# Second mixer's output: the last chunk of the first four weight tiles gets a place of its own

## The chip, the cores and the metric

One core of one Trainium2 chip. The metric is the time of one execution in device microseconds. The profile gives the span of one execution, with the activity of TensorE (PE; PEld is its weight load), VectorE (DVE), ScalarE (ACT), GpSimd (POOL), and of SyncE (SP), which only issues transfers here.

## What is computed

The reference is a network of two transformer blocks in float32 over 512 tokens of width 1024 (`D_MODEL = 1024`, `SEQ = 512`). The first block has two layers, the second one. The place of the change is the first block's second layer, whose mixer joins a multi-scale pooling with a stick-breaking attention of four heads and multiplies the result by one square matrix:

```python
def cd_mixer(h, w_in, pool_w, pool_scale, q_norm, k_norm, w_out):
    B, S, _ = h.shape
    u, sq, sk, sv = split_cols(h @ w_in, CD_SPLITS)
    o_pool = multiscale_pool(u, pool_w, pool_scale)
    q = rms_norm(sq.reshape(B, S, SB_HEADS, SB_HEAD_DIM), q_norm)
    k = rms_norm(sk.reshape(B, S, SB_HEADS, SB_HEAD_DIM), k_norm)
    v = sv.reshape(B, S, SB_HEADS, SB_HEAD_DIM)
    o_sb = stick_breaking_attention(q, k, v)
    mix = jnp.concatenate([o_pool, o_sb.reshape(B, S, -1)], axis=-1)
    return mix @ w_out
```

Then `x = x + g1 * y`, a normalisation that depends on the condition vector, and the SwiGLU feed-forward, whose first matrix is w1.

## The kernel before

**Layout.** Everything is feature-major: a chunk is 128 features (partitions) by 512 tokens, and a tensor of width 1024 is eight chunks. Products are float32 accurate by splitting each operand in an upper and a lower half and making three matmuls of each product (`products`, L391 to L393): upper weights by `hi`, upper weights by `lo`, lower weights by `hi`.

**The weight stream.** Weights come as a stream of units of 128 x 1024 floats (512 KB), in the order of use. A unit of the mixer's output matrix holds the eight 128 x 128 blocks of one output tile. SP's queue fills a ring of four places, `ring`, in order: for each unit it waits until TensorE has let go the unit four before it (`emptied`), then issues the transfer (L1273). GpSimd (`split_unit`) waits for the transfer, writes `uppers` (L1857), waits for that, and writes `lowers` over the ring's own place (L1860). TensorE waits for `lower_made`. So a ring place cannot be refilled before the last matmul that reads its lower half.

**The second mixer's output** (`second_mix_out`). Eight output tiles in two passes of four. Tile q of a pass adds up in PSUM bank q. The first pass is woven into the rest of the attention: the attention's work is cut in parts 0 to 31, which all engines go through in the same order (`sb_part(h)` on TensorE, a loop over `h` on ScalarE and VectorE). Parts 24 to 27 are each followed by chunks 0 to 3 of a tile (in the order 1, 2, 0, 3); part 28 by chunks 4 and 5 of tiles 0 and 1; part 29 by those of tiles 2 and 3; part 30 (`sb_outputs` of head 3, L518) by chunk 6 of all four, and then chunk 7 of all four, behind which each unit is let go. The second pass takes four new units, eight chunks each. Chunk 4 + n is head n's output: PSUM to SBUF on ScalarE (`cd_mixed`), then VectorE's split, `cd_split`: a cast (L2452) and a subtraction (L2453), both inside SBUF, tied to each other by a semaphore (`link`).

**VectorE's order at the end.** For head 3: the subtraction of L2473, the four products of `sb_weights` (L2480, two operands in SBUF, 128 x 128), for which TensorE's part 30 waits (`sb_w`); the split of head 3's chunk; `make_coef` (L1923, L1928, L1929: three operations on 8 columns, inside SBUF); then `residual`, over chunks k of 0 to 7: `xres` from the finished tile (L1975, one operand in PSUM); ScalarE's square and scaled copy; `raw_split` (L1936, L1937, which read PSUM); `sum_square` (L1946 or L1949).

**Behind it.** The feed-forward's first tile (`raw_tile`) starts with 16 small matmuls (L436), before which TensorE waits until seven squares are summed (`x_summed`), and then goes through the chunks as `x_raw` comes.

Of the kernel before, what the change touches and what calls it, by code (L numbers as in the profile page):

```python
# [31 lines left out]
F32 = mybir.dt.float32  # L32
F32R = mybir.dt.float32r
I32 = mybir.dt.int32
ALU = mybir.AluOpType
ACT = mybir.ActivationFunctionType
AX = mybir.AxisListType.X

P = 128
D = 1024  # L40
KC = D // P
# [5 lines left out]
RING = 4  # L47
# [91 lines left out]
def build(nc, A, plan):  # L139

    ctx = ExitStack()
    with ctx:
# [5 lines left out]
        def sem(name):  # L148
            if name not in sems:
                sems[name] = ctx.enter_context(nc.semaphore(name))  # L150
            return sems[name]
# [37 lines left out]
        def f32r(name, at, *dims):  # L189

            return nc.alloc_sbuf_tensor_at(name, [P, *dims], F32R, offset=at).ap()
# [94 lines left out]
                     ("lb", 4, S), ("w", 4, S), ("gap3", 2, S), ("u", 4, SM))  # L286
        poolw = L1["poolw"]
        B1 = L1
        cd_half = f32r("cd_half", big_at + 4 * AFTER_UPPERS, 30, S)

        def cd_mixed(k):
# [3 lines left out]
        def cd_halves(k):  # L295
            return (cd_half[:, 26 + k, :], cd_half[:, 22 + k, :]) if k < 4 else (cd_half[:, k, :], cd_half[:, k - 4, :])
# [34 lines left out]
        shift_uses = {"f0": 1, "n1": 2, "f1": 3}  # L331
        full_count = {}
        by_unit = {}

        def ready(eng, name, i=None):

            b, k = uses[name]
            if name in by_unit:
                read, n, step = by_unit[name]
                eng.wait_ge(read, n if i is None else i * step + n)  # L340
            else:
                eng.wait_ge(full[b], full_count[name])
            return b
# [19 lines left out]
        def _(pe):  # L363
# [24 lines left out]
            def products(out, s, k, hi, lo, start, stop):  # L388

                upper, lower = uppers[:, s, k * P:(k + 1) * P], lowers[:, s, k * P:(k + 1) * P]  # L390
                pe.matmul(out, upper, hi, start=start, stop=False)  # L391
                pe.matmul(out, upper, lo, start=False, stop=False)  # L392
                return pe.matmul(out, lower, hi, start=False, stop=stop)  # L393
# [145 lines left out]
            def second_mix_out():  # L539

                stream("cd_out", 0, KC)
                slot = ring_loop(2, 4)
                take = bank_loop(2, range(4), [("m1", "y", q) for q in range(4)])

                def chunks(i, q, order):
                    for k in order:
                        if i == 0:
                            pe.wait_ge(sem("m1_split"), k + 1)
                        mm = products(ps[:, q, :], (loop["base"] + q) % RING, k, *cd_halves(k), k == 0, k == KC - 1)
                    return mm  # L550
                for n, q in enumerate((1, 2, 0, 3)):
                    sb_part(24 + n)
                    take(0, q)
                    slot(0, q)
                    chunks(0, q, range(4))
                for n in range(2):
                    sb_part(28 + n)
                    for q in (2 * n, 2 * n + 1):
                        chunks(0, q, range(4, 6))
                sb_part(30)  # L560
                for q in range(4):
                    chunks(0, q, range(6, 7))
                for q in range(4):
                    chunks(0, q, range(7, 8)).then_inc(emptied[(loop["base"] + q) % RING], 1)
                for q in range(4):
                    take(1, q)
                    s = slot(1, q)
                    chunks(1, q, range(KC)).then_inc(emptied[s], 1)

            def tm_group(name, off, meta=None, first=4, between=None):  # L570

# [44 lines left out]
            def bank_loop(n_iter, banks, names, per_result=1):  # L616


                base = {}
                for n, (b, name) in enumerate(zip(banks, names)):  # L620
                    uses[name] = (b, nuse[b])
                    u = loop["base"] + (n + 1) * per_result - 1
                    by_unit[name] = (emptied[u % RING], u // RING + 1, loop["step"])
                    base[b] = nuse[b]
                    nuse[b] += n_iter

                def take(i, b):
                    pe.wait_ge(drained[b], i + base[b])
                return take
# [631 lines left out]
        @block.sync  # L1261
        def _(sp):
            for n in range(n_first):
                by = "rows" if n % ADA_FIRST >= 2 else "sums"
                sp.dma_start(first_w[n], stream_dram[n, :, :]).then_inc(sem(f"first_{by}_filled{n // ADA_FIRST}"), 16)
            sp.dma_start(small_unit, stream_dram[n_first, :, :]).then_inc(sem("small_unit_loaded"), 16)
            for s in range(RING):
                sp.dma_start(ring[:, s, :], stream_dram[n_first + 1 + s, :, :]).then_inc(filled[s], 16)
            sp.dma_start(consts[:, 0:FREQS_AT], A["consts"][:, 0:FREQS_AT]).then_inc(sem("consts_loaded"), 16)
            with sp.Fori(1, n_ring // RING) as i:  # L1270
                for s in range(RING):
                    sp.wait_ge(emptied[s], i)
                    sp.dma_start(ring[:, s, :], stream_dram[i * RING + (n_first + 1 + s), :, :]).then_inc(filled[s], 16)  # L1273
            for s in range(n_ring % RING):
                sp.wait_ge(emptied[s], n_ring // RING)
                sp.dma_start(ring[:, s, :], stream_dram[n_units - n_ring % RING + s, :, :]).then_inc(filled[s], 16)
            for k in range(KC):
                sp.wait_ge(sem("x_out"), k + 1)
                sp.dma_start(A["out"][:, k, :], hbuf[:, k, 0:S]).then_inc(sem("stored"), 16)
            sp.wait_ge(sem("stored"), 16 * KC)  # L1280

        @block.scalar
        def _(act):
# [356 lines left out]
            def sb_exps(hd, tiles, name):  # L1640

                was_drained(act, ("aft", hd, name))
                for j in tiles:
# [2 lines left out]
                        ready(act, ("so", hd - 1))  # L1646
                    f(L1["w"][:, j, 0:w], L1["lb"][:, j, 0:w], ACT.Exp).then_inc(sem("sb_e"), 1)
            for h in range(SB_ENDS):
                if h - 3 in POOL_AT:
                    g = POOL_AT.index(h - 3)  # L1650
                    b = ready(act, ("py", g))
                    drain(f(cd_mixed(g), ps[:, b, :], ACT.Copy, scale=V("pool_scale", g)), b)
                if h % 2 == 0 and h // 2 - 1 in SQK_SLOTS:
                    sqk_square(SQK_SLOTS.index(h // 2 - 1))
                if h == 12:
                    for i in range(NT):
                        b = ready(act, ("sv", i))
                        drain(f(L1["sv"][:, i, :], ps[:, b, :], ACT.Copy), b)
                if h - 2 in SB_AT:
                    hd = SB_AT.index(h - 2)  # L1660
                    sb_exps(hd, (3, 2), (3, 2))
                    sb_exps(hd, (1,), (1,))
                if h - 3 in SB_AT:
                    sb_exps(SB_AT.index(h - 3), (0,), (0,))
                if h in SB_AT:
                    sb_log(SB_AT.index(h))
                if h in SB_OUT_AT:
                    hd = SB_OUT_AT.index(h)
                    b = ready(act, ("so", hd))
                    drain(f(cd_mixed(4 + hd), ps[:, b, :], ACT.Copy), b)  # L1670
                if h % 2 and (h - 3) // 2 in SQK_SLOTS:
                    sqk_rstd(SQK_SLOTS.index((h - 3) // 2))
# [206 lines left out]
        def _(dve):  # L1879
# [597 lines left out]
            def sb_weights(hd, tiles):  # L2477
                for j in tiles:
                    dve.wait_ge(sem("sb_e"), NT * hd + NT - j)
                    tt(L1["w"][:, j, 0:P], L1["w"][:, j, 0:P], C("strict"), ALU.mult).then_inc(sem("sb_w"), 1)  # L2480
            for h in range(SB_ENDS):
                if h - 2 in SB_AT:
                    hd = SB_AT.index(h - 2)
                    sb_subtract(hd, (3, 2))
                    sb_subtract(hd, (1,))
                if h - 3 in SB_AT:
                    hd = SB_AT.index(h - 3)
                    sb_subtract(hd, (0,))
                    sb_weights(hd, (3, 2, 1, 0))
                if h - 1 in SB_AT:  # L2490
                    sb_parts(SB_AT.index(h - 1))
                if h in POOL_AT:
                    pool_window(POOL_AT.index(h))
                if h - 4 in POOL_AT:
                    g = POOL_AT.index(h - 4)
                    was_drained(dve, ("py", g))
                    cd_split(g)
                if h - 1 in SB_OUT_AT:
                    hd = SB_OUT_AT.index(h - 1)
                    was_drained(dve, ("so", hd))  # L2500
                    cd_split(4 + hd)
                if h % 2 and (h - 3) // 2 in SQK_SLOTS:
                    sqk_scale(SQK_SLOTS.index((h - 3) // 2))
# [324 lines left out]
```

## Time and profile before

| | us |
|---|---|
| median of 3 runs | 2572.9 |
| lowest, highest | 2569.6, 2574.5 |
| the profiled execution | 2572.6 |
| its span in the profile | 2570.4 |
| PE busy | 2499.6 (97%) |
| DVE, ACT, POOL busy | 1066.5, 444.1, 1687.7 |

A row of the timeline gives the start, the duration, the engine, the source line, the operation with what it writes and reads, and how many instructions of the kind are merged in it; in brackets stands how long the engine had been idle before it, and what ended that. A matmul's duration is longer than the distance to the next one, as they are pipelined; the distance is what a product costs. The granted clock of TensorE is given as a share of full speed.

### The profile page before, as it was taken

The numbers are of one execution on the slowest core, as the hardware profiler recorded it, in microseconds if no ns is written. First come the engines' busy times: TensorE is split into PE (matmuls) and PEld (weight loads), VectorE is DVE, ScalarE is ACT, GpSimd is POOL, SyncE is SP. The second block draws the span as 40 slices with busy tenths as digits, with TensorE's granted clock in tenths as the row PEclk, the third lists the DMA queues.
The fourth block names the chain that finished last, engine by engine and source line by source line (L and its number), as shares of the span: only waits on it lengthen the run. The fifth ranks groups of instructions, "written<-read, shape, count | busy, mean of one in ns | idle before, by whom it ended". The sixth has DMA issues, their size and how long they took to land.

```text
span 2570.4 us, 31432 instructions
## 1 busy us (share of the span) xinstructions
PE 2499.6 (97%) x11727; PEld 1998.7 (78%) x11727; DVE 1066.5 (41%) x1885; ACT 444.1 (17%) x872; POOL 1687.7 (66%) x789
## 2 busy tenths in 40 slices
PE   6999999999999999999999999999999999999998
PEld 3677788888887778888888678787887887888886
DVE  5897765444257463111140023204675134431322
ACT  4213420000013420000011011113543001100000
POOL 5564367777875367777877554575444787777774
PEclk9999999999999999999999999999999999999999
DMA  6323235555422122222342211221111322222222
GB/s 256 128 73 127 74 107 188 188 183 184 164 95 74 33 82 93 95 98 98 106 152 90 74 58 58 74 98 58 58 58 56 124 98 90 91 97 98 98 98 82
DMA packets 72839, 267.27 MB, mean 104 GB/s; under 512 B 8224, under 2 KB 8496, under 8 KB 72240
## 3 DMA queue, kind: packets, MB, share of 16 engines
q1 hardware_dynamic: 59760, 215.71, 24.5%
q10 hardware_dynamic: 12992, 50.34, 5.7%
q8 instruction: 63, 1.03, 0.2%
q14 instruction: 24, 0.20, 0.0%
HBM read 261.81 MB, written 4.19 MB: 103 GB/s over the span
## 4 chain that ended last, share of the span: by engine, by line
PE 85%; DVE 8%; issue 3%; ACT 1%; POOL 1%; DMA 1%; ACTq 0%; DVEq 0%; POOLq 0%; SPq 0%
PE ps L391 24%; PE ps L392 23%; PE ps L393 23%; PE ps L588 1%; PE ps L590 1%; PE ps L589 1%; DVE big L2269 1%; DVE big L2268 1%; PE ps L1080 1%; PE ps L436 1%; PE ps L598 1%; PE ps L1136 1%; PE ps L1161 1%; DVE big L2441 1%; PE ps L1045 1%
## 5 line engine op out<-in xcount | busy, mean ns | idle before, releaser
L1857 POOL TENSOR_TENSOR uppers<-ring,ones 128x1024 fp32r<-128x1024 f32 x389 | 741.7, 1907 | 802.9 <-DMA ring<-in_stream 799.5
L1860 POOL TENSOR_TENSOR lowers<-ring,uppers 128x1024 fp32r<-128x1024 f32 x389 | 939.5, 2415 | 30.5
L391 PE MATMUL ps<-x_hi,uppers 128*128 128x512 f32 x1120 | 450.2, 402 | 0.0
L393 PE MATMUL ps<-x_hi,lowers 128*128 128x512 f32 x1120 | 436.5, 390 | 0.0
L392 PE MATMUL ps<-x_lo,uppers 128*128 128x512 f32 x1120 | 436.1, 389 | 0.0
L391 PE MATMUL ps<-h_hi,uppers 128*128 128x264 f32 (+1 forms) x832 | 287.9, 346 | 5.2 <-DVE od_lo L2639 4.0
L391 PE MATMUL ps<-hid,uppers 128*128 128x512 f32 x736 | 290.1, 394 | 0.0
L393 PE MATMUL ps<-hid,lowers 128*128 128x512 f32 x736 | 286.7, 390 | 0.0
L392 PE MATMUL ps<-hid,uppers 128*128 128x512 f32 x736 | 286.4, 389 | 0.0
L392 PE MATMUL ps<-h_lo,uppers 128*128 128x264 f32 (+1 forms) x832 | 281.1, 338 | 0.0
L393 PE MATMUL ps<-h_hi,lowers 128*128 128x264 f32 (+1 forms) x832 | 280.2, 337 | 0.0
L391 PEld LDWEIGHTS ps<-x_hi,uppers 128*128 128x128 f32 x1120 | 210.4, 188 | 51.9 <-issue 9.6
L392 PEld LDWEIGHTS ps<-x_lo,uppers 128*128 128x128 f32 x1120 | 210.4, 188 | 48.4 <-issue 6.5
L393 PEld LDWEIGHTS ps<-x_hi,lowers 128*128 128x128 f32 x1120 | 210.2, 188 | 44.9
L1293 ACT ACTIVATE gate<-ps 128x512 f32<-128x512 f32 (+3 forms) x136 | 75.8, 560 | 857.9 <-PE ps L393 701.9
L391 PEld LDWEIGHTS ps<-h_hi,uppers 128*128 128x128 f32 x832 | 158.7, 191 | 34.2 <-issue 9.7
L392 PEld LDWEIGHTS ps<-h_lo,uppers 128*128 128x128 f32 x832 | 158.8, 191 | 17.8 <-issue 1.0
L393 PEld LDWEIGHTS ps<-h_hi,lowers 128*128 128x128 f32 x832 | 158.7, 191 | 16.4
L393 PEld LDWEIGHTS ps<-hid,lowers 128*128 128x128 f32 x736 | 138.1, 188 | 29.5
L392 PEld LDWEIGHTS ps<-hid,uppers 128*128 128x128 f32 x736 | 138.3, 188 | 29.0 <-issue 1.0
L391 PEld LDWEIGHTS ps<-hid,uppers 128*128 128x128 f32 x736 | 138.2, 188 | 29.0 <-issue 1.0
L2120 DVE TENSOR_TENSOR ps<-gate,ps 128x512 f32<-128x512 f32 x40 | 27.8, 696 | 282.5 <-PE ps L393 281.1
(348 smaller groups left out, 3256.1 us busy)
## 6 DMA issues: line engine op xcount, KB each, us to landing
ring<-in_stream SPq DMA_DIRECT2D x389, 512.0 KB, 3.2
sq<-in_ada_late ACTq DMA_DIRECT2D x20, 512.0 KB, 3.2
rs<-in_ada_late ACTq DMA_DIRECT2D x20, 512.0 KB, 4.7
big<-in_ada_late ACTq DMA_DIRECT2D x16, 512.0 KB, 4.4
big<-in_stream SPq DMA_DIRECT2D x13, 512.0 KB, 16.0
gate<-in_ada_rest ACTq DMA_DIRECT2D x12, 512.0 KB, 3.2
big<-in_ada_rest ACTq DMA_DIRECT2D x12, 512.0 KB, 4.1
hbuf<-in_stream SPq DMA_DIRECT2D x4, 512.0 KB, 6.7
```

The lines of the kernel that those rows point to most:

```text
L391: pe.matmul(out, upper, hi, start=start, stop=False)
L392: pe.matmul(out, upper, lo, start=False, stop=False)
L393: return pe.matmul(out, lower, hi, start=False, stop=stop)
L436: pe.matmul(ps[:, bank, 2 * (n % 2):2 * (n % 2) + 2], w[:, s, k * P:(k + 1) * P], shift_halves[:, k, :], start=k == 0 and w is uppers, sto ...
L588: pe.matmul(out, hi[:, at], upper, start=k == 0, stop=False)
L589: pe.matmul(out, hi[:, at], lower, start=False, stop=False)
L590: mm = pe.matmul(out, lo[:, at], upper, start=False, stop=k == KC - 1)
L598: pe.matmul(ps[:, b, 0:n], ones[:, :], src, start=True, stop=True).then_inc(full[b], 1)
L1293: return act.activation(out, in_, func, **kw)
L1857: pool.tensor_tensor(uppers[:, s, :], w, ones[:, 0:1].broadcast_to((P, UNIT)), ALU.mult)\
L1860: pool.tensor_tensor(lowers[:, s, :], w, uppers[:, s, :].bitcast(F32), ALU.subtract)\
L2120: tt(u, g, u, ALU.mult).then_inc(sem(st + "_hidden"), 1)
```

## The change

Four blocks of 128 x 128, chunk 7 of each of the first pass's four units, are also fetched by a transfer of their own (256 KB, pieces of 512 bytes) into `last_raw`, in a part of the memory of `u` (the pooling's input) that is free when the fourth pooling window is done. It stands in SP's queue ahead of the fill of the first of these units. ScalarE makes the upper half (in part 25), VectorE the lower (in part 26). TensorE then takes chunks 4 to 6 behind parts 28 and 29, lets each unit go there, and after part 30 takes chunk 7 of all four tiles from `last_half`. A semaphore of its own (`m1_first_y`) tells the residual that a tile of the first pass is finished. SP's loop over the fills is cut in two, and partly written out, to make room for the gather.

```diff
+        last_at = AFTER_UPPERS + 23552
+        last_raw = big[:, last_at:last_at + 4 * P].rearrange("p (a b) -> p a b", b=P)
+        last_half = f32r("last_half", big_at + 4 * (last_at + 4 * P), 2, 4, P)
...
             b, k = uses[name]
-            if name in by_unit:
+            if name in by_pass:
+                eng.wait_ge(*by_pass[name][i])
+            elif name in by_unit:
...
+                base = loop["base"]
+                gather.update(at=len_units() - KC, unit=base)
+                for q in range(4):
+                    u = base + 4 + q
+                    by_pass[("m1", "y", q)] = [(sem("m1_first_y"), q + 1), (emptied[u % RING], u // RING + 1)]
...
                 for n in range(2):
                     sb_part(28 + n)
                     for q in (2 * n, 2 * n + 1):
-                        chunks(0, q, range(4, 6))
+                        chunks(0, q, range(4, 7)).then_inc(emptied[(base + q) % RING], 1)
                 sb_part(30)
+                pe.wait_ge(sem("m1_split"), KC)
+                pe.wait_ge(sem("last_lower"), 1)
+                hi, lo = cd_halves(KC - 1)
                 for q in range(4):
-                    chunks(0, q, range(6, 7))
-                for q in range(4):
-                    chunks(0, q, range(7, 8)).then_inc(emptied[(loop["base"] + q) % RING], 1)
+                    pe.matmul(ps[:, q, :], last_half[:, 0, q, :], hi, start=False, stop=False)
+                    pe.matmul(ps[:, q, :], last_half[:, 0, q, :], lo, start=False, stop=False)
+                    pe.matmul(ps[:, q, :], last_half[:, 1, q, :], hi, start=False, stop=True).then_inc(sem("m1_first_y"), 1)
...
-            for s in range(RING):
-                sp.dma_start(ring[:, s, :], stream_dram[n_first + 1 + s, :, :]).then_inc(filled[s], 16)
+            def fill(u):
+                s = u % RING
+                if u >= RING:
+                    sp.wait_ge(emptied[s], u // RING)
+                sp.dma_start(ring[:, s, :], stream_dram[n_first + 1 + u, :, :]).then_inc(filled[s], 16)
...
-            with sp.Fori(1, n_ring // RING) as i:
-                for s in range(RING):
-                    sp.wait_ge(emptied[s], i)
-                    sp.dma_start(ring[:, s, :], stream_dram[i * RING + (n_first + 1 + s), :, :]).then_inc(filled[s], 16)
...
+            fill_all(RING, gather["unit"])
+            sp.wait_ge(sem("pooled"), 4)
+            at = gather["at"]
+            sp.dma_start(last_raw, stream_dram[at:at + 4, :, (KC - 1) * P:KC * P].rearrange("q p c -> p q c"))                .then_inc(sem("last_gathered"), 16)
+            fill_all(gather["unit"], n_ring)
...
             for h in range(SB_ENDS):
+                if h == 25:
+                    act.wait_ge(sem("last_gathered"), 16)
+                    f(last_half[:, 0, :, :], last_raw, ACT.Copy).then_inc(sem("last_upper"), 1)
...
             for h in range(SB_ENDS):
+                if h == 26:
+                    dve.wait_ge(sem("last_upper"), 1)
+                    tt(last_half[:, 1, :, :], last_raw, last_half[:, 0, :, :].bitcast(F32), ALU.subtract).then_inc(sem("last_lower"), 1)
```

## Rows read from the trace of the kernel before

**Rows 1.** The page: span, and the busy time of TensorE.

```profile
span 2570.4 us, 31432 instructions
PE 2499.6 (97%) x11727; PEld 1998.7 (78%) x11727; DVE 1066.5 (41%) x1885; ACT 444.1 (17%) x872; POOL 1687.7 (66%) x789
```

**Rows 2.** The timeline of TensorE, 894 to 943 us, the mixer's output.

```profile
894.88 0.47 PE L391 MATMUL ps<-cd_half,uppers 128*128 128x512 f32 x1
...
902.62 2.32 PE L518 MATMUL ps<-big 128*128 128x512 f32 x8
904.69 0.48 PE L391 MATMUL ps<-cd_half,uppers 128*128 128x512 f32 x1
...
916.31 0.76 PE L391 MATMUL ps<-cd_half,uppers 128*128 128x512 f32 x1 [5.91 <-POOL lowers L1860]
...
940.63 0.17 PE L436 MATMUL ps<-shift_halves,uppers 128*128 128x2 f32 x1
...
942.33 0.49 PE L391 MATMUL ps<-hid,uppers 128*128 128x512 f32 x1
```

**Rows 3.** The timeline of GpSimd behind the first pass.

```profile
911.85 1.89 POOL L1857 TENSOR_TENSOR uppers<-ring,ones 128x1024 fp32r<-128x1024 f32 x1 [33.59 <-DMA ring<-in_stream]
...
916.12 1.90 POOL L1857 TENSOR_TENSOR uppers<-ring,ones 128x1024 fp32r<-128x1024 f32 x1
```

**Rows 4.** The timelines of VectorE and ScalarE, 900 to 913 us.

```profile
900.07 0.69 DVE L2473 TENSOR_TENSOR big<-big,ps 128x512 f32<-128x512 f32 x1 [4.35 <-PE ps L507]
900.67 1.08 DVE L2480 TENSOR_TENSOR big<-big,consts 128x128 f32<-128x128 f32 x4
904.98 0.60 ACT L1293 ACTIVATE big<-ps 128x512 f32<-128x512 f32 x1 [3.55 <-PE ps L518]
905.61 0.43 DVE L2452 CAST cd_half<-big 128x512 fp32r<-128x512 f32 x1 [3.85 <-ACT big L1293]
...
908.41 0.75 DVE L1975 SCALAR_TENSOR_TENSOR xres<-ps,mod,xres 128x512 f32<-128x512 f32 x1 [1.16 <-PE ps L393]
...
912.36 0.74 DVE L1975 SCALAR_TENSOR_TENSOR xres<-ps,mod,xres 128x512 f32<-128x512 f32 x1
```

**Rows 5.** Timelines, 617 to 622 us; lines L2452, L2453 (ns min/median/max).

```profile
617.44 2.39 POOL L1860 TENSOR_TENSOR lowers<-ring,uppers 128x1024 fp32r<-128x1024 f32 x1
618.22 1.64 DVE L1923 SCALAR_TENSOR_TENSOR coef<-mod,vecs 128x8 f32<-128x8 f32 x1
619.79 1.90 POOL L1857 TENSOR_TENSOR uppers<-ring,ones 128x1024 fp32r<-128x1024 f32 x1
619.89 1.82 DVE L1928 CAST shift_halves<-mod 128x8 fp32r<-128x8 f32 x1
621.75 0.17 DVE L1929 TENSOR_TENSOR shift_halves<-mod,shift_halves 128x8 fp32r<-128x8 f32 x1
...
L2452 DVE CAST cd_half<-big x8: 420/426/2626, 801.7 to 905.6; 128x512 fp32r<-128x512 f32 x8
...
L2453 DVE TENSOR_TENSOR cd_half<-big,cd_half x8: 691/693/695, 804.4 to 906.1; 128x512 fp32r<-128x512 f32 x8
```

**Rows 6.** A hole of TensorE; two stretches (granted clock: 1.00, 0.52).

```profile
820.38 0.89 PE L504 MATMUL ps<-big,consts 128*128 128x128 f32 x4 [2.21 <-DVE big L2466]
...
820.00:824.00 4.00, 3.47 (x17) 2.80 (x18) 3.93 (x10) 0.00 (x0) 2.39 (x2) 1.00 0.21 84
914.90:921.70 6.80, 5.39 (x13) 4.28 (x14) 4.76 (x8) 1.88 (x4) 6.72 (x4) 0.52 0.15 61
```

**Rows 7.** Timelines where the additions go; a unit's transfer (us).

```profile
879.21 0.63 ACT L1293 ACTIVATE big<-big 128x512 f32<-128x512 f32 x1 [4.51 <-DVE big L2473]
...
884.76 0.29 DVE L2462 SCALAR_TENSOR_TENSOR big<-ps,big 128x128 f32<-128x128 f32 x1 [2.89 <-ACT big L1293]
...
ring<-in_stream SPq DMA_DIRECT2D x389, 512.0 KB, 3.2
```

More of the change, by code:

```diff
@@ L288, in build @@
         B1 = L1
+        last_at = AFTER_UPPERS + 23552
+        assert L1["u"].offset == big[:, last_at:].offset, (L1["u"].offset, big[:, last_at:].offset)
+        last_raw = big[:, last_at:last_at + 4 * P].rearrange("p (a b) -> p a b", b=P)
+        last_half = f32r("last_half", big_at + 4 * (last_at + 4 * P), 2, 4, P)
         cd_half = f32r("cd_half", big_at + 4 * AFTER_UPPERS, 30, S)
@@ L333, in build @@
         by_unit = {}
+        by_pass = {}
+        gather = {}
         def ready(eng, name, i=None):
             b, k = uses[name]
-            if name in by_unit:
+            if name in by_pass:
+                eng.wait_ge(*by_pass[name][i])
+            elif name in by_unit:
                 read, n, step = by_unit[name]
@@ L548, in chunks @@
                             pe.wait_ge(sem("m1_split"), k + 1)
-                        mm = products(ps[:, q, :], (loop["base"] + q) % RING, k, *cd_halves(k), k == 0, k == KC - 1)
+                        mm = products(ps[:, q, :], (base + q) % RING, k, *cd_halves(k), k == 0, k == KC - 1)
                     return mm
@@ L568, in second_mix_out, with len_units @@
                     chunks(1, q, range(KC)).then_inc(emptied[s], 1)
+            def len_units():
+                return sum(count for _, _, count in units)
             def tm_group(name, off, meta=None, first=4, between=None):
@@ L1266, in _, with fill_all @@
             sp.dma_start(small_unit, stream_dram[n_first, :, :]).then_inc(sem("small_unit_loaded"), 16)
-            for s in range(RING):
-                sp.dma_start(ring[:, s, :], stream_dram[n_first + 1 + s, :, :]).then_inc(filled[s], 16)
-            sp.dma_start(consts[:, 0:FREQS_AT], A["consts"][:, 0:FREQS_AT]).then_inc(sem("consts_loaded"), 16)
-            with sp.Fori(1, n_ring // RING) as i:
-                for s in range(RING):
-                    sp.wait_ge(emptied[s], i)
-                    sp.dma_start(ring[:, s, :], stream_dram[i * RING + (n_first + 1 + s), :, :]).then_inc(filled[s], 16)
-            for s in range(n_ring % RING):
-                sp.wait_ge(emptied[s], n_ring // RING)
-                sp.dma_start(ring[:, s, :], stream_dram[n_units - n_ring % RING + s, :, :]).then_inc(filled[s], 16)
+            def fill(u):
[3 more added lines that the diff above has]
+                sp.dma_start(ring[:, s, :], stream_dram[n_first + 1 + u, :, :]).then_inc(filled[s], 16)
+            def fill_all(u, end):
+                while u < end and (u < RING or u % RING):
+                    fill(u)
+                    u += 1
+                rounds = (end - u) // RING
+                if rounds:
+                    with sp.Fori(u // RING, u // RING + rounds) as i:
+                        for s in range(RING):
+                            sp.wait_ge(emptied[s], i)
+                            sp.dma_start(ring[:, s, :], stream_dram[i * RING + (n_first + 1 + s), :, :]).then_inc(filled[s], 16)
+                    u += rounds * RING
+                while u < end:
+                    fill(u)
+                    u += 1
+            fill_all(0, RING)
+            sp.dma_start(consts[:, 0:FREQS_AT], A["consts"][:, 0:FREQS_AT]).then_inc(sem("consts_loaded"), 16)
+            fill_all(RING, gather["unit"])
[3 more added lines that the diff above has]
+            fill_all(gather["unit"], n_ring)
             for k in range(KC):
```

## The prediction, made before the change was run

> **What bounds the kernel now.** I read the page first: TensorE is busy in 97% of 2570.4 us [rows 1]. So a gain has to come out of a hole in TensorE's row, and a loss from a new one. Then I read TensorE's timeline through the output of the second mixer [rows 2]. The first output pass (four tiles, chunks 0 to 7) ends with chunk 6 from 904.69 and chunk 7, whose last product is issued at about 904.69 + 24 x 0.2275, that is 910.1. The next one starts at 916.31, behind 5.91 us without work that end with GpSimd's `lowers`. GpSimd's timeline says why [rows 3]: it had waited 33.59 us for a DMA, split the first refilled unit from 911.85, and began the next at 916.12, 4.27 us a unit. Its units are let go only at the last product of chunk 7: VectorE picks up the first finished tile at 908.41 [rows 4], so 3.44 us pass from the release to the start of the split and 4.3 more to the product. The hole costs more than itself: in the stretch behind it the granted clock is 0.52, the lower of the two levels (1.2 GHz), and products come 0.43 us apart in place of 0.2275 [rows 6]. The second pass has 96 products, 21.9 us at full clock, and takes 916.31 to 940.63, 24.3 us [rows 2]. So the hole costs 5.9 + 2.4 = 8.3 us, and that is the most that removing it can give.
>
> **The change, part by part.** *The early release.* Chunk 6 now lies in parts 28 and 29, and each unit is let go behind it. The parts start at 894.88 as before. Tile 0 has nine products there, so its unit is free at about 894.9 + 9 x 0.2275 + 0.2, that is 897.2, not 908.4. With the same 3.44 us GpSimd starts at 900.65 in place of 911.85, and the other three releases (the last at about 905.7) are early enough to keep it busy: four units by 4.3 us, without a stop until 917.8 at least. All units of the second pass are then there when TensorE wants them. That the products and their number are the same is plain from the code.
>
> *Chunk 7 loses its cover.* It needs head 3's output, split by VectorE. Part 30 (`sb_outputs` of head 3) moves behind the 12 products of chunk 6: 902.62 + 2.73 = 905.35. From its start to the end of the split it was 905.61 + 0.43 + 0.69 - 902.62 = 4.1 us, of which TensorE works 2.07 (902.62 to 904.69) [rows 2, 4]; chunk 6 used to fill the other 2.0 and now nothing does. In the bare order chunk 7 runs 909.5 to 912.3, and tile 0 reaches VectorE at 908.41 + 2.1 = 910.5.
>
> *The residual chain becomes the bound.* From 908.41 the chain goes VectorE, ScalarE, VectorE in steps of 912.36 - 908.41 = 3.95 us for one tile [rows 4]. TensorE's shift products at the head of the feed-forward (L436) wait for the sum over seven of the eight, so for 7 x 3.95 = 27.7 us behind the chain's start. Before, that would have been 936.1, and TensorE came at 940.63 [rows 2]: 4.5 us of slack. With a bare start at 910.5 the sum is there at 938.2, while the second pass ends at 912.3 + 21.9 = 934.2. The hole of 8.3 us has turned into one of 2.1 us and one of 4.0 us, and of the gain 2.4 us are left.
>
> *GpSimd's port against VectorE's tail.* Now GpSimd splits from 900.65 to 918, exactly while VectorE does the last pieces; before it was idle there [rows 3]. Rows 5 show what that does. GpSimd ran 617.44 to 619.8 and 619.79 to 621.69. VectorE's L1923, an operation on 8 columns with two inputs in SBUF, took 1.64 us and ended with GpSimd's instruction; L1928, a small cast inside SBUF, took 1.82 and ended with the next; L1929, in the crack between two, took 0.17. L2452, the very cast of this tail, has a median of 0.426 and a longest of 2.626 us. A waiting VectorE operation thus gets in when GpSimd's present instruction ends, but the next GpSimd instruction is then ahead of VectorE's next. Operations with one input in PSUM show none of it: the chain's step is the same 3.95 under GpSimd's work from 911.85 on [rows 3, 4].
> Exposed are the four `sb_w` products (L2480), L2452, L2453, and L1923, L1928, L1929 of `make_coef`, which is queued ahead of the residual. I step through it with GpSimd's 1.90 and 2.39 in turn. The L2480 would begin at 900.67 + 1.37 = 902.05 and get in at 902.6. If all four then go through together (to 903.5), part 30 is not late and ScalarE's copy, which began 2.36 us behind the part's start (904.98 less 902.62) and took 0.60, ends at 908.3. GpSimd's next three run 903.5 to 905.9, to 907.8 and to 910.25: L2452 waits until 910.25 and ends 910.65; L2453 stands behind one more (913.2, where chunk 7 starts), L1923 behind one more (915.75), L1928 behind one (917.7), L1929 slips in, and the chain starts at 917.9. If GpSimd gets in between each of the four, `sb_w` is ready at 910.0, part 30 starts there, chunk 7 at 917.4, and L1923 gets in when GpSimd's eighth instruction ends, at 919.8; then GpSimd has nothing left, and the chain starts at 920.4. The two ends lie close because both are held by the same eight instructions. No row shows which, so I take the middle, 919.1. The sum of seven is ready at 919.1 + 27.7 = 946.8 against 940.63: +6.2 us. Even in the later order chunk 7 ends by 921 and pass two by some 945 with slow products, so TensorE waits for the chain, not for itself.
> The Trainium skill (SBUF — State Buffer, section "SBUF: two separate sides") has VectorE and GpSimd share a port pair under an exclusive lock held for a whole instruction, and counts VectorE's operations with two SBUF inputs among those that need it. By that L2453 is exposed. L2453's own row, 691 to 695 ns in all eight executions [rows 5], shows no wait; L1923's does. By L2453's own row alone the chain would start some 2.4 us earlier and the time would be 2.4 us less than my forecast.
>
> *The clock behind the new hole.* A hole of 5.9 us was followed by 0.52 [rows 2, 6], one of 2.21 us, ended at 820.38, left the clock at 1.00 [rows 6]. The new one before L436 is over 4 us long in every version, so I charge the 2.4 us again, at 946.8; the old one's 2.4 are already inside 940.63. From below, if the short products take the slow time, it is 0; from above 2.7 (half of the 5.4 us at low clock that followed 916.31).
>
> *At nothing:* the gather of 256 KB, half a unit (a unit lands in 3.2 us [rows 7]), on SP's queue ahead of the fill of the pass's first unit, which is not used before 886; its wait for the fourth window is on something that the queue has passed by then, and behind it only fills wait, for units that TensorE takes later. If that cover were gone, it is 2 to 3 us once. ScalarE's copy (0.6 us) lies in an idle 4.51 before 879.21, VectorE's subtraction (0.7) in an idle 2.89 before 884.76, with GpSimd idle [rows 3, 7]; uncovered they would cost 0.6 and 0.7. The unrolled SP queue costs TensorE nothing, since the fills are early.
>
> Sum: 2572.6 (this execution's own time, 0.3 below the median of 2572.9) + 6.2 + 2.4 = 2581.2.
>
> **Rivals.** *A, no port conflict in the tail.* Chain start 910.5, sum at 938.2: -2.4, and the clock +2.4 behind a hole of 4.0: 2572.6, no change. For it: L2453's row, and most L2452. Against it: rows 5, and GpSimd's 17 us without a stop. With only the cast held the start moves to some 911.5 to 914 and the time to 2574 to 2577. *B, faster.* The second pass follows chunk 7 and L436 follows it at once: 934.2 against 940.63, so 2566.2. The mechanism is a residual chain that keeps up; it decides from a step of (934.2 - 910.5)/7 = 3.4 us down. The step of 3.95 speaks against it. *C, the release brings nothing,* because a queue holds the fills: SP takes them in order and has nothing but emptied slots ahead, so 2572.6 + 2.1 for the lost cover of chunk 7, at little chance.
>
> **How the numbers follow.** Forecast (a tail held by GpSimd, both orders) 0.74: 2580.0 with the four together, 2582.5 with GpSimd in between each. A with its partial form 0.20, C 0.03, B 0.03. A measurement here tells 0.2%, 5.1 us, from no change. The forecast lies above that in both orders; A and C lie within it; B lies outside on the other side. So faster 0.03, same 0.23, slower 0.74. The range goes from A's partial form, 2574, to the later order with the larger clock loss and something for the ends, 2584.5.
>
> **What the profile after would show.** GpSimd's split from about 900.7 on with at most cracks in it. L2452, L2453, L1923 and L1928 at 1 to 2.7 us each in place of 0.43, 0.69, 0.16, 0.17, and L2480 long or not, which settles the order. TensorE without work before chunk 7, by 2.1 us if the tail is free and 6 or more if not; no wait for `lowers` in the second pass; a new wait at L436 for VectorE's sum, and a clock of about 0.5 behind it. Wrong would be the prediction if the L1975 of chunk 0 starts before 913 (then the chain is not late), if the step is under 3.95, or if the clock stays at 1.00 behind the wait.

## The result

Over 12 runs each the changed kernel has a median of 2576.9 us, the kernel before 2571.1. The medians are 5.8 us apart; the ratio on record is 1.0026 with a 95% interval of 1.0014 to 1.0038, that is slower by 6.7 us, 3.6 to 9.8. The forecast was +8.6 us (2581.2 against 2572.6), in a range of 2574.0 to 2584.5.

From here on I measure the *stage*: from the first product of part 28 to the first product of the square sum in the feed-forward's first tile (L421, L429 after the change). It took 945.20 - 894.88 = 50.3 us before and takes 59.4 us after. TensorE does the same work in it in every kernel below, and what lies before and behind it varies from execution to execution. Each value of the stage comes from one profiled execution, with what the clock did in it.

TensorE's timeline of the changed kernel, answering to [rows 2] (products are now L399 to L401, the new chunk 7 is L578 to L580, part 30 is L526, the shift products L444):

```profile
900.99 0.48 PE L399 MATMUL ps<-cd_half,uppers 128*128 128x512 f32 x1
...
913.48 2.39 PE L526 MATMUL ps<-big 128*128 128x512 f32 x8 [1.87 <-DVE big L2520]
...
920.54 0.80 PE L578 MATMUL ps<-cd_half,last_half 128*128 128x512 f32 x1 [4.67 <-DVE cd_half L2493]
...
952.65 0.34 PE L444 MATMUL ps<-shift_halves,uppers 128*128 128x2 f32 x1 [5.16 <-DVE big L1989]
...
956.06 0.77 PE L399 MATMUL ps<-hid,uppers 128*128 128x512 f32 x1
...
960.38 1.02 PE L429 MATMUL ps<-big,ones 128*128 128x512 f32 x2
```

The wait of 5.91 us for GpSimd before the second pass is gone. Three waits for VectorE stand in its place: 1.87 us before part 30, 4.67 before chunk 7, 5.16 before the shift products. The two engines behind them, GpSimd first [rows 3], then VectorE [rows 4]:

```profile
906.79 1.90 POOL L1897 TENSOR_TENSOR uppers<-ring,ones 128x1024 fp32r<-128x1024 f32 x1 [22.49 <-DMA ring<-in_stream]
908.76 2.52 POOL L1900 TENSOR_TENSOR lowers<-ring,uppers 128x1024 fp32r<-128x1024 f32 x1
911.24 1.94 POOL L1897 TENSOR_TENSOR uppers<-ring,ones 128x1024 fp32r<-128x1024 f32 x1
913.26 2.35 POOL L1900 TENSOR_TENSOR lowers<-ring,uppers 128x1024 fp32r<-128x1024 f32 x1
915.57 1.89 POOL L1897 TENSOR_TENSOR uppers<-ring,ones 128x1024 fp32r<-128x1024 f32 x1
917.54 2.40 POOL L1900 TENSOR_TENSOR lowers<-ring,uppers 128x1024 fp32r<-128x1024 f32 x1
919.90 2.34 POOL L1897 TENSOR_TENSOR uppers<-ring,ones 128x1024 fp32r<-128x1024 f32 x1
922.32 2.38 POOL L1900 TENSOR_TENSOR lowers<-ring,uppers 128x1024 fp32r<-128x1024 f32 x1
```

```profile
908.14 5.19 DVE L2520 TENSOR_TENSOR big<-big,consts 128x128 f32<-128x128 f32 x4
916.54 1.20 DVE L2492 CAST cd_half<-big 128x512 fp32r<-128x512 f32 x1 [3.21 <-ACT big L1330]
917.78 2.71 DVE L2493 TENSOR_TENSOR cd_half<-big,cd_half 128x512 fp32r<-128x512 f32 x1
920.41 1.85 DVE L1963 SCALAR_TENSOR_TENSOR coef<-mod,vecs 128x8 f32<-128x8 f32 x1
922.30 0.17 DVE L1968 CAST shift_halves<-mod 128x8 fp32r<-128x8 f32 x1
922.50 2.22 DVE L1969 TENSOR_TENSOR shift_halves<-mod,shift_halves 128x8 fp32r<-128x8 f32 x1
924.65 0.74 DVE L2015 SCALAR_TENSOR_TENSOR xres<-ps,mod,xres 128x512 f32<-128x512 f32 x1
...
928.60 0.74 DVE L2015 SCALAR_TENSOR_TENSOR xres<-ps,mod,xres 128x512 f32<-128x512 f32 x1
```

Read the ends together. GpSimd's instruction of 915.57 ends at 917.46 and the cast at 917.74; the one of 917.54 ends at 919.94 and the subtraction at 920.49; the one of 919.90 ends at 922.24 and the 8-column L1963 at 922.26. Each of these three VectorE operations gets in where GpSimd changes instruction, and the next one of VectorE is then behind GpSimd's next. The residual's first L2015 stands 23.7 us into the stage; before it was at 13.5.

The clock in three stretches (the seventh figure), answering to [rows 6]: chunk 7, the wait before L444, and what follows it. The low clock of chunk 7 costs nothing in the end, as TensorE waits for the chain later on.

```profile
920.50:924.90 4.40, 4.36 (x10) 3.47 (x11) 4.33 (x5) 0.00 (x0) 4.12 (x2) 0.50 0.00 0
947.40:952.60 5.20, 0.10 (x1) 0.00 (x0) 3.89 (x7) 1.21 (x2) 3.81 (x3) 0.98 0.31 101
952.60:959.30 6.70, 6.65 (x24) 6.00 (x25) 1.84 (x3) 1.21 (x2) 2.81 (x2) 0.50 0.00 0
```

The stage is 9.1 us longer, but the profiled span only 4.9 (2575.3 against 2570.4), because other things differ between the two profiled executions. The stage itself starts at 900.99 against 894.88. That is not the gather: e2 and e4 below have it too and start the stage at 895.25 and 894.73. Over all ten kernels profiled here it starts anywhere from 894.7 to 903.7, the latest in a kernel whose work up to there is that of before (e6). Behind the stage the kernel before needs 1625.2 us and the changed one 1614.9. In the second block there are two stretches that the one execution ran partly at the lower clock and the other did not; first the kernel before, then the changed one:

```profile
1780.00:1795.00 15.00, 13.66 (x58) 10.19 (x54) 4.79 (x15) 5.47 (x14) 1.43 (x1) 0.66 0.10 35
1961.00:1971.00 10.00, 8.72 (x49) 8.49 (x50) 3.25 (x7) 2.68 (x5) 0.00 (x0) 0.66 0.09 23
```

```profile
1789.00:1804.00 15.00, 15.00 (x104) 11.93 (x103) 8.94 (x30) 7.82 (x19) 6.51 (x4) 1.00 0.21 70
1970.00:1980.00 10.00, 8.81 (x73) 8.63 (x74) 3.50 (x8) 2.68 (x5) 0.00 (x0) 1.00 0.16 54
```

Two stretches at 0.66, 15 and 10 us long, are up to 5.1 and 3.4 us less progress. Of the ten kernels profiled only this execution shows the first of them, so I take it for a difference between executions; the medians over 12 runs average over it, the single spans do not.

### The profile page after: what moved, and what is told of

It is laid out like the page before. It is cut to its first block, busy times and chain, and to the rows that moved or that the text cites. A ratio compares the mean times of both kernels' runs of the same rounds, so it can differ in the third digit from the quotient of the medians.

```text
span 2575.3 us, 31426 instructions
## 1 busy us (share of the span) xinstructions
PE 2503.3 (97%) x11727; PEld 1999.4 (78%) x11727; DVE 1082.7 (42%) x1886; ACT 444.9 (17%) x873; POOL 1688.1 (66%) x789
## 4 chain that ended last, share of the span: by engine, by line
PE 88%; DVE 7%; issue 2%; ACT 2%; POOL 1%; DMA 1%; ACTq 0%; DVEq 0%; POOLq 0%; SPq 0%
PE ps L399 24%; PE ps L400 24%; PE ps L401 24%; PE ps L607 2%; PE ps L608 2%; PE ps L609 2%; PE ps L1099 1%; PE ps L444 1%; PE ps L617 1%; PE ps L1155 1%; PE ps L1180 1%; DVE big L2481 1%; PE ps L1064 1%; DMA xres<-in_x 1%; ACT big L1330 1%
## 5 line engine op out<-in xcount | busy, mean ns | idle before, releaser
L399 PE MATMUL ps<-x_hi,uppers 128*128 128x512 f32 x1120 | 451.8, 403 | 0.0
L401 PE MATMUL ps<-x_hi,lowers 128*128 128x512 f32 x1120 | 437.3, 390 | 0.0
L399 PE MATMUL ps<-h_hi,uppers 128*128 128x264 f32 (+1 forms) x832 | 285.6, 343 | 5.6 <-DVE od_lo L2682 4.2
L399 PE MATMUL ps<-hid,uppers 128*128 128x512 f32 x736 | 290.9, 395 | 0.0
L401 PE MATMUL ps<-hid,lowers 128*128 128x512 f32 x736 | 287.2, 390 | 0.0
L401 PE MATMUL ps<-h_hi,lowers 128*128 128x264 f32 (+1 forms) x832 | 278.1, 334 | 0.0
L399 PEld LDWEIGHTS ps<-x_hi,uppers 128*128 128x128 f32 x1120 | 211.3, 189 | 52.6 <-issue 10.4
L401 PEld LDWEIGHTS ps<-x_hi,lowers 128*128 128x128 f32 x1120 | 211.1, 188 | 45.1
L399 PEld LDWEIGHTS ps<-h_hi,uppers 128*128 128x128 f32 x832 | 156.5, 188 | 33.8 <-issue 9.0
L401 PEld LDWEIGHTS ps<-h_hi,lowers 128*128 128x128 f32 x832 | 156.4, 188 | 16.4
L401 PEld LDWEIGHTS ps<-hid,lowers 128*128 128x128 f32 x736 | 138.5, 188 | 29.5
L399 PEld LDWEIGHTS ps<-hid,uppers 128*128 128x128 f32 x736 | 138.7, 188 | 29.1 <-issue 1.0
```

## The experiments

The question was which of two theories holds. Theory 1: GpSimd's early split holds VectorE's tail, and the residual chain carries the delay to L444. Theory 2: the tail and the chain are late only because chunk 7 lost its cover, and GpSimd has no part. All times in the table come from the profiles, one execution each, counted from the stage's start; the ratio is to the kernel before, run beside it. No ratio is more than 0.3% from 1, and stage and whole time do not agree to the microsecond: the whole times of e1, e2 and e7 fell by 4.9, 7.2 and 5.4 us, their stages by 2.0, 3.5 and 2.5.

| kernel | residual starts | L436/L444 starts | stage | ratio to before, 95% |
|---|---|---|---|---|
| before | 13.5 | 45.8 | 50.3 | |
| changed | 23.7 | 51.7 | 59.4 | 1.0026 (1.0014 to 1.0038) |
| e1, GpSimd held | 15.6 | 43.7 | 48.3 | 0.9981 (0.9966 to 0.9995) |
| e2, release behind part 30 | 13.5 | 42.3 | 46.8 | 0.9972 (0.9958 to 0.9986) |
| e3, make_coef early | 21.2 | 49.2 | 55.4 | 1.0013 (1.0001 to 1.0025) |
| e4, split from PSUM | 21.0 | 49.0 | 57.5 | 1.0022 (1.0012 to 1.0032) |
| e5, short chain | 23.7 | 48.1 | 52.7 | 1.0014 (1.0002 to 1.0026) |
| e6, short chain in before | 13.5 | 45.8 | 50.3 | 1.0003 (0.9990 to 1.0017) |
| e7, tile 0 early | 13.6 | 41.6 | 47.8 | 0.9979 (0.9963 to 0.9995) |
| e8, e7 with short chain | 13.6 | 38.8 | 43.4 | 0.9973 (0.9960 to 0.9987) |

**e1: the changed kernel, with GpSimd held until VectorE's tail is through.**

```diff
+            held = gather["unit"] + 4
...
+            for n in range(RING):
+                if rest + RING * i0 + n == held:
+                    pool.wait_ge(sem("shift_split"), 3)
+                split_unit(rest + RING * i0 + n)
```

GpSimd's loop over the units is cut around the held one.

> I measure the stage from the first product of part 28 to the first product of the square sum in the feed-forward's first tile: 50.3 us in the kernel before, 59.4 in the changed one. Here GpSimd does not split the first refilled unit until make_coef is done; nothing else differs from the changed kernel. Theory 1 (GpSimd's split holds VectorE's tail through the shared port): the four sb_w products, the cast, the subtraction and the coefficient operations fall back to 0.28, 0.43, 0.69 and 0.17 us; TensorE waits 2.0 us before chunk 7 and about 2 before the second pass; L1975's counterpart of chunk 0 starts some 15.6 us into the stage instead of 23.7, the stage takes about 51 us and the time is some 8 us below the changed kernel's, about that of before. Theory 2 (the loss is chunk 7's lost cover and the residual chain; GpSimd has no part): the tail's durations stay as they are, the units come later, and the stage takes 59.4 us or more.

VectorE's tail in e1, and TensorE's waits:

```profile
904.43 1.08 DVE L2529 TENSOR_TENSOR big<-big,consts 128x128 f32<-128x128 f32 x4
910.72 0.43 DVE L2501 CAST cd_half<-big 128x512 fp32r<-128x512 f32 x1 [5.21 <-ACT big L1330]
911.18 0.69 DVE L2502 TENSOR_TENSOR cd_half<-big,cd_half 128x512 fp32r<-128x512 f32 x1
911.79 0.16 DVE L1972 SCALAR_TENSOR_TENSOR coef<-mod,vecs 128x8 f32<-128x8 f32 x1
...
912.93 0.75 DVE L2024 SCALAR_TENSOR_TENSOR xres<-ps,mod,xres 128x512 f32<-128x512 f32 x1 [0.56 <-PE ps L580]
```

```profile
911.93 0.50 PE L578 MATMUL ps<-cd_half,last_half 128*128 128x512 f32 x1 [1.88 <-DVE cd_half L2502]
...
916.92 0.72 PE L399 MATMUL ps<-cd_half,uppers 128*128 128x512 f32 x1 [1.97 <-POOL lowers L1900]
...
940.94 0.24 PE L444 MATMUL ps<-shift_halves,uppers 128*128 128x2 f32 x1 [0.40 <-DVE big L1998]
```

Every operation has its bare duration, and nothing was done but to let GpSimd start later. The units' transfers still ran under the tail (209 GB/s from 907.00 to 912.00), so it is not they that held it. Theory 2 falls. The lost cover of chunk 7 by itself is the 1.88 us. The stage came out at 48.3 us, not at the 51 expected: the second pass still waits 1.97 us for its unit, and the clock falls behind that hole, short as it is:

```profile
916.90:921.00 4.10, 4.08 (x11) 3.24 (x12) 2.79 (x6) 1.21 (x2) 4.02 (x2) 0.58 0.00 0
```

At 0.58 over 4.1 us that costs 1.7 us, in time in which TensorE would have waited for the chain anyway. TensorE comes to L444 later and waits only 0.40 us there, and the clock is full from there on. This kernel is faster than before, by the interval 1.3 to 8.7 us.

**e2: chunk 6 behind part 30 again, the units let go there.**

```diff
-                        chunks(0, q, range(4, 7)).then_inc(emptied[(base + q) % RING], 1)
+                        chunks(0, q, range(4, 6))
                 sb_part(30)
+                for q in range(4):
+                    chunks(0, q, range(6, 7)).then_inc(emptied[(base + q) % RING], 1)
```

> Chunk 6 goes back behind part 30 and the units are let go there; chunk 7 still comes from last_half. Both theories have chunk 6 cover the split again, so the residual starts 13.5 us into the stage as in the kernel before. Theory 1 has GpSimd start at about 14.2 us, behind the tail, so that no VectorE operation is long; the hole before the second pass is about 3.1 us in place of 5.9, the sum for L436 is ready at 41.3 us, and the stage takes 46 us, or 47.5 if the clock falls in the hole: 3 to 4.5 us below the kernel before. Theory 2 gives the same for this one; if GpSimd's port had held nothing, and the loss were somewhere in the gather or the added halves, the stage would be longer than before's 50.3.

GpSimd starts at 14.3 us (909.58), 1.9 us behind VectorE's tail. The hole before the second pass is 3.26 us, and the clock did fall behind it, as the stretch after it shows:

```profile
914.04 0.47 PE L399 MATMUL ps<-cd_half,uppers 128*128 128x512 f32 x1 [3.26 <-POOL lowers L1902]
```

```profile
914.00:921.00 7.00, 6.96 (x24) 5.59 (x25) 4.89 (x8) 1.94 (x4) 6.84 (x4) 0.76 0.00 0
```

At 0.76 over 7 us it costs 1.7 us. The stage, 46.8 us, lies between the two values expected. Giving up most of the earlier release gains, where the whole of it loses.

**e3: the changed kernel, `make_coef` moved into VectorE's part 26.**

```diff
                 if h == 26:
+                    make_coef(V("ffn_norm", KC, KC), 1, 3)
                     dve.wait_ge(sem("last_upper"), 1)
...
-            make_coef(V("ffn_norm", KC, KC), 1, 3)
             residual("m1", "f1", 1, 2, raw=lambda k: (raw_hi[:, k, :], raw_lo[:, k, :]))
```

> The changed kernel with make_coef moved into VectorE's part 26. Theory 1: three operations fewer stand in the held tail; the residual starts when tile 0 is finished, 2.4 us earlier than in the changed kernel, and the stage takes 57.0 us in place of 59.4. Theory 2: what is saved is their bare length, 0.5 us.

```profile
905.53 5.14 DVE L2520 TENSOR_TENSOR big<-big,consts 128x128 f32<-128x128 f32 x4
913.88 1.20 DVE L2492 CAST cd_half<-big 128x512 fp32r<-128x512 f32 x1 [3.21 <-ACT big L1330]
915.11 2.71 DVE L2493 TENSOR_TENSOR cd_half<-big,cd_half 128x512 fp32r<-128x512 f32 x1
919.56 0.75 DVE L2015 SCALAR_TENSOR_TENSOR xres<-ps,mod,xres 128x512 f32<-128x512 f32 x1 [1.74 <-PE ps L580]
```

The products, the cast and the subtraction are held as in the changed kernel, and the residual starts when tile 0 is finished, 2.5 us earlier. That is five times the bare length of what was moved. The stage fell by 4.0 instead of 2.4, as the hole before L444 shrank to 2.9 us and less time went by at the lower clock behind it.

**e4: the changed kernel, head 3's chunk split straight from PSUM.**

```diff
+                        b = ready(dve, ("so", hd))
+                        hi, lo = cd_halves(4 + hd)
+                        link(dve.tensor_copy(hi, ps[:, b, :]))
+                        drain(tt(lo, ps[:, b, :], hi.bitcast(F32), ALU.subtract), b)
```

ScalarE's copy of this head is left out, and a memset of one column gives the signal that `cd_split` gave.

> The changed kernel, but head 3's chunk is split by VectorE straight from PSUM, without ScalarE's copy: both operations have an input in PSUM. Theory 1: they take 0.7 us each although GpSimd is at work, chunk 7 starts 3.1 us earlier, the residual 2.2 to 4.4 us earlier (the coefficient operations are still held), and the stage takes 55 to 57 us. Theory 2: saved are 0.6 of the copy less 0.3 of the slower cast, 0.3 us.

```profile
911.37 0.69 DVE L2550 CAST cd_half<-ps 128x512 fp32r<-128x512 f32 x1 [4.26 <-PE ps L526]
912.09 0.69 DVE L2551 TENSOR_TENSOR cd_half<-ps,cd_half 128x512 fp32r<-128x512 f32 x1
912.83 0.87 DVE L1964 SCALAR_TENSOR_TENSOR coef<-mod,vecs 128x8 f32<-128x8 f32 x1
...
913.74 1.82 DVE L1969 CAST shift_halves<-mod 128x8 fp32r<-128x8 f32 x1
```

Under the same GpSimd work the cast and the subtraction take 0.69 us each; of the three operations behind them, inside SBUF, two are held still. Chunk 7 starts 1.3 us earlier, not 3.1: behind a hole of 1.89 us the clock fell in part 30, whose eight products took 4.08 us in place of 2.39.

```profile
907.25 4.08 PE L526 MATMUL ps<-big 128*128 128x512 f32 x8 [1.89 <-DVE big L2521]
```

```profile
907.20:911.30 4.10, 4.05 (x8) 2.27 (x8) 0.00 (x0) 0.00 (x0) 4.03 (x2) 0.58 0.23 90
```

The residual starts 2.7 us earlier and L444 too. The stage is only 1.9 us shorter, a little outside the 55 to 57 expected: the wait before L444 is still 5.1 us, and 8.6 us pass from L444 to the square sum, against 7.7 in the changed kernel and 4.6 at full clock.

**e5 and e6: ScalarE's two operations of the residual exchanged, in the changed kernel and in the one before.**

```diff
             for k in range(KC):
-                square("f1", "m1", k)
+                x_chunk(act, "m1", k)
                 scale("f1", k, coef)
+                square("f1", "m1", k)
```

`x_chunk` is the wait for the finished `xres`, which now stands ahead of the scaled copy.

> The changed kernel with ScalarE's two operations of the residual of this stage in the other order: first the scaled copy, on which VectorE waits, then the square. If the residual chain is what sets L436 (L444 there), its step falls from 3.95 to about 3.4 us, the sum of seven is ready 23.9 us behind the chain's start instead of 27.7, and the stage takes 55 to 55.5 us in place of 59.4. If TensorE itself or the held tail alone set it, the stage stays at 59.4.

> The same exchange of ScalarE's two operations in the kernel before. There the chain had 4.5 us of slack and TensorE came to L436 last, so both theories expect the stage to stay at 50.3 us and the time within 0.1% of before's. A shorter stage would mean that the chain bound that kernel as well.

In e5 the steps begin at 920.08, 923.50, 926.94:

```profile
920.08 0.74 DVE L2016 SCALAR_TENSOR_TENSOR xres<-ps,mod,xres 128x512 f32<-128x512 f32 x1
...
923.50 0.74 DVE L2016 SCALAR_TENSOR_TENSOR xres<-ps,mod,xres 128x512 f32<-128x512 f32 x1
```

```profile
944.52 0.24 PE L444 MATMUL ps<-shift_halves,uppers 128*128 128x2 f32 x1 [1.44 <-DVE big L1990]
```

A step of 3.43 us in place of 3.95 brings L444 3.6 us forward in the changed kernel and nothing, 45.76 against 45.75, in the one before. So the chain had slack before and was the bound after. Behind the remaining wait of 1.44 us the clock stayed at 1.00 (944.00 to 949.20), which gives another 3.1 us in this execution; so the stage took 52.7 us, less than the 55 to 55.5 expected.

**e7 and e8: chunk 6 of tile 0 alone ahead of part 30,** `make_coef` early, and in e8 the short chain.

```diff
-                        chunks(0, q, range(4, 7)).then_inc(emptied[(base + q) % RING], 1)
+                        chunks(0, q, range(4, 6))
+                chunks(0, 0, range(6, 7)).then_inc(emptied[base % RING], 1)
                 sb_part(30)
+                for q in range(1, 4):
+                    chunks(0, q, range(6, 7)).then_inc(emptied[(base + q) % RING], 1)
```

> Chunk 6 of tile 0 alone goes ahead of part 30 and lets its unit go there; chunk 6 of tiles 1 to 3 stays behind part 30 as cover and lets its units go; make_coef in part 26. GpSimd should start its split some 12.0 us into the stage, when VectorE's tail is over (its subtraction ends at 12.5), so theory 1 has no held operation; the second pass starts at about 16.8 us behind a hole of 1.5, too short for the clock to fall; but the residual starts at 13.5 and its sum is ready at 41.2, so L436 waits for it about 2.5 us and the stage takes 45.8 us: 4.5 us below before. If GpSimd's start catches the tail after all, the residual starts 2 to 4 us later and the stage takes 48 to 50.

> The kernel of e7 with the short chain of e5: the sum is ready at 37.4 us, before TensorE needs it at 38.7, so only the hole of 1.5 us is left. The stage takes 43.3 us, 7 us below before, and the time is 0.997 of before's or a little less. If the clock falls in the hole of 1.5 us, 45.5 us.

In both GpSimd starts 12.0 to 12.1 us into the stage, while the last operation of the tail is in, and it is GpSimd that waits (here e8, 2.33 us in place of 1.90):

```profile
913.32 0.69 DVE L2497 TENSOR_TENSOR cd_half<-big,cd_half 128x512 fp32r<-128x512 f32 x1
```

```profile
913.44 2.33 POOL L1901 TENSOR_TENSOR uppers<-ring,ones 128x1024 fp32r<-128x1024 f32 x1 [28.74 <-DMA ring<-in_stream]
```

e7's L444 came as worked out (41.6 us, behind a wait of 2.69), but the clock fell, so the stage was 47.8 and not 45.8:

```profile
942.00:945.40 3.40, 3.40 (x10) 2.64 (x10) 0.62 (x1) 0.00 (x0) 2.86 (x2) 0.57 0.00 0
```

e8 has only the hole of 1.29 us before the second pass, and its stage was 43.35 us against 43.3 expected: 7.0 less than before. Its ratio, 0.9973 (0.9960 to 0.9987), is 6.9 us. It beats the kernel before and the changed one; between e2, e7 and e8 the whole times do not decide. Their stages, one execution each, put e8 first, and would do so without the clock: e2 and e7 lost 1.7 and about 1.6 us to it.

## Why the prediction was right, point by point

**The gain that was to be had** came as worked out. GpSimd started its split 5.8 us into the stage, forecast 5.8, and TensorE never waited for it in the second pass.

**The lost cover of chunk 7**, forecast 2.0 us, measured 1.88 where it stands alone (e1).

**The conflict with GpSimd** is shown by e1: without GpSimd's work at that time the tail is short. That it lies in operands inside SBUF is shown by e4 for the cast and the subtraction. Only the order within it was between my two. Of the four `sb_w` products two went through together, and the third and the fourth each stood behind an instruction of GpSimd: 5.19 us, where the two cases had about 1.4 and 8. The cast waited only for the rest of GpSimd's fifth instruction (it took 1.20 us, where the case worked out had 2.3), the subtraction for a whole one (2.71). Of the three coefficient operations the second slipped through and not the third. The residual started at 23.7 us against 24.2 forecast (919.1 less 894.88). The forecast was the middle of two orders, and the true order was neither; that it hit within 0.5 us is partly luck. That GpSimd holds the tail is not.

**L2453, the subtraction.** Its own eight executions before, all of 0.69 us, spoke against its being held. It took 2.71 us in the changed kernel. The eight short ones had never met GpSimd at work in front of them: ahead of seven GpSimd stood idle, also behind the three casts that had been held (2.63, 2.61 and 1.70 us), and the eighth, at 834.99, was in first, so that GpSimd's instruction of 835.19 took 2.25 us in place of 1.89. By the Trainium skill (SBUF — State Buffer, section "SBUF: two separate sides") an operation with two inputs in SBUF needs the shared pair; the 2.71 us agree with it.

**The residual chain** was the bound with its step of 3.95 us (924.65 to 928.60); L444 stood 51.7 us into the stage, forecast 51.9. e5 and e6 show that it bound the changed kernel and not the one before.

**The clock** behind the last hole, forecast 2.4 us, cost 3.1 (7.7 us from L444 to the square sum, 4.6 at full clock). The forecast took the cost from 96 long products and left out what the 16 short shift products lose at the lower clock: they are 0.21 us apart, 3.4 us for all, where they were 0.11 apart and took 1.7 [rows 2].

So the stage is 9.1 us longer (5.9 for the chain, 3.2 for the clock) where the sum said 8.6 (6.2 and 2.4). The whole time moved by 6.7, and its interval holds both. The median, 2576.9, is 4.3 us below the forecast's 2581.2: 1.5 of it is the base (2572.6 against 2571.1), the rest is not settled. The profiled execution of before had lost several microseconds to the clock elsewhere, and in the changed kernel's the clock fell behind a hole of 2.26 us ahead of the stage.

**Rival A** had the right condition, no conflict in the tail, and the wrong price. With the conflict taken away (e1) the time was not the same but 0.19% below before: its hole of 4 us before L436, and the clock's 2.4 us, did not come, because there GpSimd's units were late again: TensorE waited 1.97 us before the second pass instead and lost 1.7 us to the clock behind that. Whether A's own form, an early split and a free tail, would have had them was not tried; no kernel here has both. **Rival B** needed a step of 3.4 us; e5 has 3.43, and with the held tail that makes a slower kernel still. With the free tail (e8 against e7) it takes the stage from 47.8 to 43.4. **Rival C** fell: the release took effect at once.

## What to carry to other kernels

Before moving GpSimd's work earlier, look at what VectorE does in the time that it moves into: here operations with two inputs in SBUF and casts inside SBUF stood behind GpSimd's instructions, most of them one by one, and the price went by GpSimd's instructions, not by the size of VectorE's. Two of the three operations on 8 columns (1.85 and 2.22 us; the third slipped through in 0.17) cost about as much as those of 512 (1.20 and 2.71), so move them away (e3), or split from PSUM (e4), where both halves kept their 0.69 us. And a stall taken from one engine is only gained as far as the chain behind it has slack: here 4.5 of 8.3 us, until its step was shortened.

## What was not expected of the hardware

Two `sb_w` products in a row got in together between two GpSimd instructions (around 908.7, where one instruction ended at 908.69 and the next, from 908.76, took 2.52 us in place of 2.40), the other two one at a time, so the turns are not strictly one and one. The length of a hole in TensorE's work did not settle by itself whether the clock fell. Inside the stage it kept 1.00 behind holes of 1.26, 1.29, 1.44, 1.64, 1.82, 1.87 and 1.88 us, but fell behind 1.89 (e4) and 1.97 (e1), and behind every one from 2.69 us up. The hole at 820.38 [rows 6], from which the prediction reads that 2.21 us leave the clock alone, is in all ten profiles, 2.21 to 2.26 us long: behind it the clock stayed at 1.00 in four (before, e1, e2, e4) and fell in six, the changed kernel among them:

```profile
824.78 0.89 PE L512 MATMUL ps<-big,consts 128*128 128x128 f32 x4 [2.26 <-DVE big L2506]
```

```profile
824.80:832.40 7.60, 7.46 (x26) 5.59 (x27) 5.81 (x11) 1.14 (x3) 4.27 (x2) 0.78 0.04 16
```

So the same hole of some 2.2 us can cost nothing or a stretch at the lower clock, and a stage read from one execution holds that chance. What sets it no run here shows. A hole that is made shorter can give back the clock, as in e5 against the changed kernel, which has 3.6 us from the chain and 3.1 from the clock.
